# Delta rule by half blocks: the triangular inverse in 64 × 64 tiles, the pair loop unrolled and its order changed

## Chip, cores and metric

One core of one Trainium2 chip. The metric is the device time of one execution in microseconds (us); 0.2% of it, about 2.3 us, is what a measurement of this kernel can tell from no change.

## What is computed

Two transformer layers and a hybrid layer on 256 tokens of width 1024, all in float32. The change lies in one part of the hybrid layer, the gated delta rule (8 heads of 128):

```
q, k, v = silu(causal_dwconv(h @ w_q | h @ w_k | h @ w_v))    # four taps
g = -exp(a_log) * softplus(decay + dt);  beta = sigmoid(beta_logit)
q = l2norm(q) * dk ** -0.5;  k = l2norm(k);  G = cumsum(g)
m  = strict_lower((beta * k) @ k.T * exp(G_i - G_j))
sol = triangular_solve(m + I, [beta * v, beta * exp(G) * k])
u, w = sol
qk = lower(q @ k.T * exp(G_i - G_j))
# scan over chunks c:
v_new = u - w @ state;  o = exp(G) * q @ state + qk @ v_new
state = state * exp(G_last) + (k * exp(G_last - G)).T @ v_new
# then: rmsnorm(o, gain) * silu(z) @ w_branch_b
```

The kernel works in chunks of 128 tokens, two chunks per head, so that for each head two matrices I + m of 128 × 128 are inverted.

## The kernel before

Every projection splits a float32 weight chunk of 128 × 1024 into a high part (ScalarE, L343) and a low part (VectorE or GpSimd, L354, `raw - high`), and TensorE takes three matmuls of 256 columns (high·xh, high·xl, low·xh) for each 128 × 128 block: 24 matmuls make one projected block of 128 channels × 256 tokens. The delta rule's blocks are written at L1572 (`gdn_block`), in two parts of 12. Block (x, e) is query (x = 0), key (1), value (2) or gate z (3) of head e of a pair. ScalarE takes its last tap (L1587), VectorE adds three taps (L1607), ScalarE makes a tanh (L1598) into an SBUF buffer, and VectorE multiplies the two SBUF buffers to the silu (L1617). A gate block needs only a tanh (L1592) and one product (L1627). All low parts of this phase are GpSimd's.

The heads go in four pairs. `pair_pe` for pair i has two stages.

- **Levels.** The inverse is built by doubling: starting from blocks of 2, six levels each multiply M by the inverse (`level_x`, L1809, 4 matmuls, one for each of the pair's four matrices, into bank A[0]); VectorE masks it (`level_xm`, L1822); TensorE multiplies the masked product from both sides (`level_t`, L1816 and L1817, 8 matmuls into A[2] and A[3]); VectorE subtracts (`level_tt`, L1827, 1024 columns; L1830 at the last level). The inverse and its transpose are kept, each 128 × 512. A plain float32 matmul is two passes on TensorE, so that the trace shows 8 and 16 instructions. Behind each of the 12 groups stands half a block of the next pair: (0,0), (1,0), (2,0), (0,1), (1,1), (2,1) in the 12 gaps.
- **Tail.** The transposes of the next pair's queries and keys (`turn_pe`, L1640), the recurrence f1 to f4 (L1847 to L1879), and between its steps the blocks (3,0) and (3,1), the next pair's values transposed (L1647), the normed queries and keys turned back (`back_pe`, L1655), their products (L1667), the pair's result transposed (L1891), the next M transposed (L1676), and last `spin(pe, A[1], 4)`: four matmuls of 512 columns on constants (L491) whose result nobody reads.

Between them runs a chain over the other engines for the next pair: squares (ScalarE, L1682), their sums (VectorE, L1713), the root (GpSimd, `root_pool`, L1766), a factor and the normed rows (VectorE, `norm_dve`: L1732, L1734), back, copies (ScalarE, L1694), products, masks (VectorE, L1754), first inverse (GpSimd, `init_pool`: L1796, L1799; and VectorE, `init_dve`: L1761, L1762). The pair's own result norm (L2035, root at L2098, L2040, transpose, L2048) stands in the tail too. Each engine works its list in order. For the last pair the gaps hold attention's first projections (L2159, L2171). `gdn_pe` and its like are the ramp: the first pair's eight blocks, with the gates, before pair 0.

The pairs run as first pair, a hardware loop over the middle (`over`), last pair.

Of the kernel before, what the change touches and what calls it, by code (L numbers as in the profile page):

```python
# [19 lines left out]
ALU = mybir.AluOpType  # L20
# [3 lines left out]
P = 128  # L24
TOK = 256
# [17 lines left out]
LEVELS = 6  # L43

# [67 lines left out]
for _n, _w in (("ident", P), ("upper", P), ("strict_lower", P), ("level1", P), ("level1_t", P),  # L112
               ("levels", LEVELS * P), ("ones", P), ("causal", 3 * P), ("dist", NT * TOK),
               ("mla_cos", NT * MLA_ROPE), ("mla_sin", NT * MLA_ROPE), ("mla_rot", TOK),
               ("att_cos", NT * 2 * ROT), ("att_sin", NT * 2 * ROT)):
    _const(_n, _w)
# [3 lines left out]
def constants():  # L120
# [12 lines left out]
    def level(s):  # L133
        return (r // (2 * s) == k // (2 * s)) & (r % (2 * s) >= s) & (k % (2 * s) < s)

    put("level1", level(1))
    put("level1_t", level(1).T)
    put("levels", np.stack([level(2 << n) for n in range(LEVELS)], 1))
# [112 lines left out]
def build(nc, dram, y_out):  # L251
# [66 lines left out]
    def repeat(ap, n):  # L318

        return ap.unsqueeze(1).to_broadcast([P, n, ap.shape[1]])  # L320
# [1199 lines left out]
    tanh_ = [sb(f"tanh{x}", [P, TOK]) for x in range(4)]  # L1520
# [11 lines left out]
    qk_t = silu2[:, 0:4, :].rearrange("p (e x) (c k) -> p e (x c) k", e=2, c=2)  # L1532
    qdec_t = sb("qdec_t", [P, 2, P])
# [4 lines left out]
    inv = sb("inv", [P, 2, 4, P])  # L1538
    bm = sb("bm", [P, 2, 4, P])
    dcum = bm[:, 0, :, :]  # L1540
    xm = sb("xm", [P, 4, P])
# [10 lines left out]
    level_of = cst("levels", "p (l k) -> p l k", l=LEVELS)  # L1552
    BLOCKS = [(0, 0), (1, 0), (2, 0), (0, 1), (1, 1), (2, 1)]
# [5 lines left out]
    def gdn_block(pe, x, e, j, part):  # L1559
# [3 lines left out]
        if part == 0:  # L1563
            chunk_ready(pe, p, slot, c)
            if not (isinstance(b_, int) and b_ == 0):
                pe.wait_ge(taps[x]["tap"], 3 * b_ if x < 3 else b_)
            elif x == 3:
                pe.wait_ge(z_["dve"], 10)
# [7 lines left out]
    def block_act(act, split, x, e, j):  # L1576
        block_mid_act(act, split, x, e, j)
        block_end_act(act, x, e, j)

    def block_mid_act(act, split, x, e, j):  # L1580
# [3 lines left out]
        if x < 3:  # L1584
            if not (isinstance(b_, int) and b_ == 0):
                act.wait_ge(taps[x]["silu"], b_)
            act.activation(conv[x][:], W[x][:, 0:TOK], ACT.Copy, scale=conv_tap(b_, x, 3)).then_inc(taps[x]["mid"], 1)  # L1587
            refill(split, p, slot, c)
        else:
            if not (isinstance(b_, int) and b_ == 0):  # L1590
                act.wait_ge(taps[x]["tap"], b_)
            act.activation(tanh_[x][:], W[x][:, 0:TOK], ACT.Tanh, scale=0.5).then_inc(taps[x]["th"], 1)  # L1592
            refill(split, p, slot, c)

    def block_end_act(act, x, e, j):
        if x < 3:
            act.wait_ge(taps[x]["tap"], 3 * (2 * j + e) + 3)
            act.activation(tanh_[x][:], conv[x][:], ACT.Tanh, scale=0.5).then_inc(taps[x]["th"], 1)  # L1598
# [13 lines left out]
    def block_silu_dve(dve, x, e, j):  # L1612
        b_ = 2 * j + e
        dve.wait_ge(taps[x]["th"], b_ + 1)
        if (x, e) == BLOCKS[0] and not is0(j):
            dve.wait_ge(e_["grown"], j)
        dve.scalar_tensor_tensor(silu2[:, 3 * e + x, :], tanh_[x][:], 1.0, conv[x][:], ALU.add, ALU.mult).then_inc(taps[x]["silu"], 1)  # L1617

    def block_dve(dve, x, e, j):
        b_ = 2 * j + e  # L1620
        if x < 3:
            block_taps_dve(dve, x, e, j)
            block_silu_dve(dve, x, e, j)
        else:
            dve.wait_ge(taps[x]["th"], b_ + 1)
            dst = z2[:, b_, :] if isinstance(b_, int) else z2[:, bass.ds(b_, 1), :].rearrange("p a k -> p (a k)")
# [1104 lines left out]
```

## Time and profile before

| | us |
|---|---|
| median of 3 runs (1140.10 to 1142.44) | 1141.54 |
| profiled execution, own time | 1142.67 |
| its span in the trace | 1140.8 |
| TensorE busy (95% of the span) | 1084.0 |
| VectorE busy (61%) | 695.8 |
| ScalarE busy (49%) | 560.6 |
| GpSimd busy (37%) | 427.7 |
| mean granted TensorE clock | 0.988 |

The profiled execution is 1.1 us over the median. Busy time counts each record from start to its modelled end; matmuls overlap, so starts are the better measure of their cost. In the trace's lines a float32 matmul counts as two instructions; PEld is the weight load.

### The profile page before, as it was taken

Reading aid. Unit: us, or ns where it says so; the run is one execution under the profiler, and the core shown is the slowest. Engines: PE = TensorE matmul, PEld = TensorE weight load, DVE = VectorE, ACT = ScalarE, POOL = GpSimd, SP = SyncE. Lnnn points to the kernel's source line nnn. Section 1 sums busy time; section 2 is a strip of 40 time slices with the busy share of each in tenths; the row PEclk is TensorE's granted clock in tenths of the full one; section 3 lists DMA queues with packets and bytes.
Section 4 is the critical chain, followed back from the end, with each engine's and each line's share of the span. In section 5 each row is a group of like instructions: output and inputs, shape, how many; then the busy total and the mean of one; then the engine's idle time right before and its main releaser. Section 6 shows DMA issues by size and latency. Waiting matters only on the chain.

```text
span 1140.8 us, 21023 instructions
## 1 busy us (share of the span) xinstructions
PE 1084.0 (95%) x7774; PEld 991.4 (87%) x7774; DVE 695.8 (61%) x1054; ACT 560.6 (49%) x1022; POOL 427.7 (37%) x295
## 2 busy tenths in 40 slices
PE   9799999999999998999999987999999999999997
PEld 7699689999969986799999876888898989999996
DVE  3555776776676556677676666666667455544444
ACT  4455665555555555655555554233323245544442
POOL 1000233334332331333334636546564345534331
PEclk9999999999999999999999998999999999999999
DMA  8234366555435422555564323131220324446551
GB/s 341 84 110 137 129 206 217 185 186 182 148 130 169 147 96 109 200 190 184 177 208 160 130 95 112 45 104 49 100 82 29 120 85 148 153 142 204 184 183 38
DMA packets 46129, 162.43 MB, mean 142 GB/s; under 512 B 5248, under 2 KB 5504, under 8 KB 45952
## 3 DMA queue, kind: packets, MB, share of 16 engines
q1 hardware_dynamic: 44784, 157.05, 41.3%
q0 software_dynamic: 1296, 4.72, 1.3%
q8 instruction: 32, 0.52, 0.2%
q14 instruction: 17, 0.14, 0.0%
HBM read 160.70 MB, written 1.05 MB: 142 GB/s over the span
## 4 chain that ended last, share of the span: by engine, by line
PE 83%; DVE 9%; ACT 3%; issue 2%; POOL 2%; DMA 0%; DVEq 0%; POOLq 0%; ACTq 0%
PE work L385 13%; PE work L387 13%; PE work L386 13%; PE acc L385 5%; PE acc L386 5%; PE acc L387 5%; PE work L1572 5%; PE work L2159 4%; PE work L2171 2%; PE acc L1809 2%; DVE silu L1617 2%; PE acc L1817 2%; PE acc L2171 1%; DVE conv L1607 1%; PE acc L1816 1%
## 5 line engine op out<-in xcount | busy, mean ns | idle before, releaser
L354 POOL TENSOR_TENSOR low<-raw,high 128x1024 fp32r<-128x1024 f32 x109 | 265.3, 2436 | 328.3 <-ACT high L343 328.3
L354 DVE TENSOR_TENSOR low<-raw,high 128x1024 fp32r<-128x1024 f32 (+3 forms) x183 | 271.1, 1489 | 163.7 <-ACT high L343 163.5
L343 ACT ACTIVATE high<-raw 128x1024 fp32r<-128x1024 f32 (+2 forms) x293 | 300.1, 1032 | 44.0 <-DMA raw<-in_w_out 22.1
L385 PE MATMUL work<-xh,high 128*128 128x256 f32 (+1 forms) x1032 | 292.3, 283 | 0.7 <-DVE low L354 0.7
L386 PE MATMUL work<-xl,high 128*128 128x256 f32 (+1 forms) x1032 | 289.4, 280 | 0.0
L387 PE MATMUL work<-xh,low 128*128 128x256 f32 (+1 forms) x1032 | 289.1, 280 | 0.0
L385 PEld LDWEIGHTS work<-xh,high 128*128 128x128 f32 (+1 forms) x1032 | 194.5, 188 | 7.6 <-issue 4.8
L386 PEld LDWEIGHTS work<-xl,high 128*128 128x128 f32 (+1 forms) x1032 | 194.8, 189 | 2.3 <-issue 0.6
L387 PEld LDWEIGHTS work<-xh,low 128*128 128x128 f32 (+1 forms) x1032 | 194.8, 189 | 0.2
L1110 POOL TENSOR_TENSOR h<-gelu,cv 128x256 f32<-128x256 f32 x44 | 48.8, 1108 | 200.6 <-ACT gelu L1030 106.8
L1572 PE MATMUL work<-xh,high 128*128 128x256 f32 x256 | 77.2, 301 | 3.4 <-DVE conv L1607 1.7
L1572 PE MATMUL work<-xl,high 128*128 128x256 f32 x256 | 72.4, 283 | 0.0
L1572 PE MATMUL work<-xh,low 128*128 128x256 f32 x256 | 72.3, 282 | 0.0
L385 PE MATMUL acc<-high,hh 128*128 128x512 f32 x168 | 65.9, 392 | 1.2 <-DVE low L354 1.2
L386 PE MATMUL acc<-low,hh 128*128 128x512 f32 x168 | 65.8, 392 | 0.0
L387 PE MATMUL acc<-high,hl 128*128 128x512 f32 x168 | 65.4, 389 | 0.0
L1036 ACT ACTIVATE hh<-h 128x256 fp32r<-128x256 f32 x44 | 18.4, 418 | 70.1 <-POOL h L1110 70.1
L1572 PEld LDWEIGHTS work<-xh,high 128*128 128x128 f32 x256 | 49.3, 193 | 4.0 <-issue 3.1
L1024 ACT ACTIVATE cv<-work,vec 128x256 f32<-128x256 f32 x44 | 24.8, 564 | 51.0 <-PE work L387 51.0
L1572 PEld LDWEIGHTS work<-xl,high 128*128 128x128 f32 x256 | 49.3, 192 | 0.0
L1572 PEld LDWEIGHTS work<-xh,low 128*128 128x128 f32 x256 | 49.0, 191 | 0.0
L1112 POOL TENSOR_TENSOR hl<-h,hh 128x256 fp32r<-128x256 f32 x44 | 34.0, 773 | 24.4 <-ACT hh L1036 24.4
(376 smaller groups left out, 2345.5 us busy)
## 6 DMA issues: line engine op xcount, KB each, us to landing
raw<-in_w_ffn SPq DMA_DIRECT2D x132, 512.0 KB, 4.2
raw<-in_w_out SPq DMA_DIRECT2D x39, 512.0 KB, 4.1
raw<-in_w_diff SPq DMA_DIRECT2D x32, 512.0 KB, 4.2
raw<-in_w_att SPq DMA_DIRECT2D x32, 512.0 KB, 3.9
raw<-in_w_gdn SPq DMA_DIRECT2D x24, 512.0 KB, 3.7
raw<-in_w_mla SPq DMA_DIRECT2D x8, 512.0 KB, 3.3
raw<-in_w_gdnz SPq DMA_DIRECT2D x8, 512.0 KB, 5.0
raw<-in_w_mla SPq DMA_DIRECT2D x8, 384.0 KB, 3.2
```

The costliest lines, as they stand in the source:

```text
L343: act.activation(high[k][:, 0:w], raw[k][:, 0:w], ACT.Copy).then_inc(high_done[k], 1)
L354: eng.tensor_tensor(low[k][:, 0:w], raw[k][:, 0:w], high[k][:, 0:w], ALU.subtract).then_inc(low_done[k], 1)
L385: pe.matmul(out, lhs[0], rhs[0], start=start, stop=False)
L386: pe.matmul(out, lhs[0], rhs[1], start=False, stop=False)
L387: return pe.matmul(out, lhs[1], rhs[0], start=False, stop=stop)
L1024: act.activation((cg, cv)[value][j][:], W[bank][:, 0:TOK], ACT.Identity, scale=ffn_taps(layer, i, j, value, 1, 0), bias=ffn_taps(layer, i, ...
L1110: pool.tensor_tensor(h32[j][:], gelu[j][:], cv[j][:], ALU.mult).then_inc(s["h32"], 1)
L1112: pool.tensor_tensor(hl[j][:], h32[j][:], hh[j][:], ALU.subtract).then_inc(s["hl"], 1)
L1572: last = pe.matmul(W[x][:, 0:TOK], l[slot][:, b * P:(b + 1) * P], r[:, b, :], start=(s == 0), stop=(s == 23))
L1617: dve.scalar_tensor_tensor(silu2[:, 3 * e + x, :], tanh_[x][:], 1.0, conv[x][:], ALU.add, ALU.mult).then_inc(taps[x]["silu"], 1)
L2159: last = pe.matmul(W[0][:, t * TOK:(t + 1) * TOK], x[:, b, t * P:(t + 1) * P], w[k][:, o:o + TOK], start=(b == 0 and term == 0), stop=(b = ...
L2171: last = pe.matmul(out, w[k][:, b * P:(b + 1) * P], x[:, b, :], start=(s == 0), stop=(s == 23))
```

## The change

1. The inverse's diagonal 64 × 64 blocks are built alone. `inv` shrinks from 128 × 2 × 4 × 128 to 128 × 2 × 4 × 64, both halves on their own partitions. In `level_x` and `level_t` each 128 × 128 × 128 matmul becomes two of 64 × 64 × 64 (rows and outputs on partitions 0 to 63, and on 64 to 127). Five levels go that way; a last one makes the off-diagonal 64 × 64 block, with 4 + 4 matmuls of that size, into `inv_t`, the full transposed inverse. Products of both sides go into one bank.
2. Order on TensorE: gaps hold (0,0), (1,0), (0,1), (1,1), (3,0), (2,0). `turn_pe` moves up to gap 9, ahead of the last level. Values are transposed at gap 2 of the pair's own levels, the result of the pair before at gap 5. The tail holds block (3,1) (between f1 and f3), `back_pe` behind f2, products behind f3, `turn_m_pe` and then block (2,1). The spin is gone; the ramp's last spin is 2 instead of 4.
3. VectorE: the result norm's three steps move to levels 1, 2 and 3 or 4 of the next pair, scaled keys and values to levels 0 and 4, z's products and the masks to the tail. `init_pool` becomes VectorE's `init_rows_dve`. The taps stand between a level's two VectorE steps, the silu behind the second.
4. The tanh of a query, key or value block is written to the free half of the block's own PSUM bank; the next block in that bank then waits for the silu, not for the taps.
5. Pairs are unrolled in Python on all engines; the weight loads on the sync queue are written out in the new order.

```diff
 def gdn_block(pe, x, e, j, part):
-                pe.wait_ge(taps[x]["tap"], 3 * b_ if x < 3 else b_)
+            elif x < 3:
+                pe.wait_ge(taps[x]["silu"], b_)
...
-            act.activation(tanh_[x][:], conv[x][:], ACT.Tanh, scale=0.5).then_inc(taps[x]["th"], 1)
+        act.activation(W[x][:, TOK:2 * TOK], conv[x][:], ACT.Tanh, scale=0.5).then_inc(taps[x]["th"], 1)
...
 def level_x(pe, l, j):
         for c in range(4):
-            last = pe.matmul(A[0][:, c * P:(c + 1) * P], mt[:, c, :], inv[:, 0, c, :], start=True, stop=True)
+            at = slice(c * HALF, (c + 1) * HALF)
+            if l < LEVELS - 1:
+                for h_ in HALVES:
+                    last = pe.matmul(A[0][h_, at], mt[h_, c, h_], inv[h_, 0, c, :], start=True, stop=True)
+            else:
+                last = pe.matmul(A[0][upper, at], mt[lower, c, upper], inv[lower, 0, c, :], start=True, stop=True)
 def level_t(pe, l, j):
-                pe.matmul(A[2][:, c * P:(c + 1) * P], inv[:, 1, c, :], xm[:, c, :], start=True, stop=True)
-            last = pe.matmul(A[3][:, c * P:(c + 1) * P], xm[:, c, :], inv[:, 1, c, :], start=True, stop=True)
+                for h_ in HALVES:
+                    pe.matmul(A[2][h_, at], inv[h_, 1, c, :], xm[h_, c, :], start=True, stop=True)
+                for h_ in HALVES:
+                    last = pe.matmul(A[2][h_, at_t], xm[h_, c, :], inv[h_, 1, c, :], start=True, stop=True)
+            else:
+                last = pe.matmul(A[2][lower, at], xm[upper, c, :], inv[upper, 1, c, :], start=True, stop=True)
 def level_tt(dve, l, j):
+            if l == LEVELS - 2:
+                dve.wait_ge(e_["tt"], LEVELS * j + l + 1)
+                for h_ in HALVES:
+                    dve.tensor_copy(inv_t[h_, :, h_], inv[h_, 1, :, :])
+def init_rows_dve(dve, j):
+        for h_ in HALVES:
+            last = dve.tensor_tensor(bm[h_, 0, :, 0:HALF]..., mk[h_, :, 0, :, h_], level1..., ALU.mult)
+        dve.tensor_tensor(inv[:, 0, :, :], repeat(cst("ident_half"), 4), bm[:, 0, :, 0:HALF], ALU.subtract)
+def gap_pe(pe, i, gap):
+            gdn_block(pe, *GAP_BLOCKS[gap // 2], i + 1, gap % 2)      # attention's gaps for the last pair
+        if gap == 2:
+            turn_values_pe(pe, i)
+        if gap == 5 and i > 0:
+            turn_result_pe(pe, i - 1)
+        if gap == 9 and not last_pair:
+            turn_pe(pe, i + 1)
 def pair_pe(pe, i):                     # tail, more pairs to come
-            gdn_block(pe, 3, 0, i + 1, 0)
+            gdn_block(pe, 3, 1, i + 1, 0)         # behind f1
-            gdn_block(pe, 3, 0, i + 1, 1)
+            back_pe(pe, i + 1)                    # behind f2
+            gdn_block(pe, 3, 1, i + 1, 1)
-            turn_values_pe(pe, i + 1)
-            back_pe(pe, i + 1)
+            products_pe(pe, i + 1)                # behind f3
-            gdn_block(pe, 3, 1, i + 1, 0)
-            products_pe(pe, i + 1)
-            gdn_block(pe, 3, 1, i + 1, 1)
+            turn_m_pe(pe, i + 1)                  # behind f4
+            for part in range(2):
+                gdn_block(pe, 2, 1, i + 1, part)
-            turn_m_pe(pe, i + 1)
-            spin(pe, A[1], 4)
 def pair_pool(pool, i):
+            root_pool(pool, i + 1)
+            block_low_pool(split, 3, 0, i + 1)
+            block_low_pool(split, 2, 0, i + 1)
+            pool.wait_ge(e_["init_g"], i + 2)
+            grow_pool(pool, i + 1)
+            block_low_pool(split, 3, 1, i + 1)
+            block_low_pool(split, 2, 1, i + 1)
+        else:
+            refill(split, ph["att"], 0, 0)
+            result_root_pool(pool, i - 1)
```

## Rows read from the trace of the kernel before

**Rows 1.** Windows: ramp, pair 0, pair 1; start:end, length, busy (count) by engine, clock, DMA.
```profile
668.10:717.90 49.80, 40.29 (x284) 36.27 (x283) 34.51 (x52) 25.50 (x42) 31.42 (x19) 0.93 0.24 85
717.90:774.30 56.40, 52.82 (x413) 49.51 (x412) 36.72 (x57) 19.37 (x35) 27.87 (x20) 0.97 0.23 75
774.30:829.20 54.90, 51.25 (x413) 47.93 (x413) 36.74 (x57) 19.38 (x35) 30.98 (x21) 1.00 0.24 77
```

**Rows 2.** TensorE's waits in pairs 1 and 2 (774 to 883.5 us): total, times, longest.
```profile
PE work L1647 <- DVE silu L1617: 3.8, 2, 1.9
PE work L1655 <- DVE qk_tok L1734: 1.5, 2, 0.7
PE acc L1809 <- DVE inv L1762: 1.1, 2, 0.6
```

**Rows 3.** TensorE's timeline, one level of pair 1: start, length, engine, line, tiles, shapes, count.
```profile
785.66 1.16 PE L1809 MATMUL acc<-inv,mt 128*128 128x128 f32 x8
786.58 0.36 PE L1572 MATMUL work<-xh,high 128*128 128x256 f32 x1
...
788.07 0.38 PE L1816 MATMUL acc<-xm,inv 128*128 128x128 f32 x2
...
789.78 0.36 PE L1572 MATMUL work<-xh,high 128*128 128x256 f32 x1
...
791.33 0.38 PE L1809 MATMUL acc<-inv,mt 128*128 128x128 f32 x1
```

**Rows 4.** TensorE's timeline: matmuls with 64 weight rows (L1199) and their neighbours; 128 rows (L856).
```profile
406.78 1.06 PE L1231 MATMUL work<-v_sb,prob_t 128*128 128x128 f32 x8
407.76 1.13 PE L1199 MATMUL work<-k_sb,q_pair 64*128 64x256 f32 x8
...
409.05 0.28 PE L386 MATMUL work<-xl,high 128*128 128x256 f32 x1
```
```profile
40.98 0.59 PE L856 MATMUL work<-kr_t,qr_t 128*128 128x256 f32 x2
41.42 0.59 PE L855 MATMUL work<-k_sb,q_sb 128*128 128x256 f32 x2
```

**Rows 5.** Line L1199 in 407.70 to 407.80 us: durations in ns, first and last start.
```profile
L1199 PE MATMUL work<-k_sb,q_pair x2: 480/480/480, 407.8 to 407.8; 64*128 64x256 f32 x2
```

**Rows 6.** TensorE's timeline: the closest starts of two full-size matmuls.
```profile
38.46 0.22 PE L385 MATMUL work<-high,ckh 128*128 128x128 f32 x1
38.52 0.28 PE L386 MATMUL work<-low,ckh 128*128 128x128 f32 x1
```

**Rows 7.** TensorE's timeline, end of pair 1's tail.
```profile
825.03 3.60 PE L491 MATMUL acc<-const 128*128 128x512 f32 x8
829.19 1.16 PE L1809 MATMUL acc<-inv,mt 128*128 128x128 f32 x8 [0.56 <-DVE inv L1762]
```

**Rows 8.** VectorE's timeline in pair 1's tail.
```profile
810.10 1.22 DVE L1713 TENSOR_REDUCE ssq<-sq 128x8 f32<-128x1024 f32 x1 [2.00 <-ACT sq L1682]
...
813.43 2.41 DVE L1617 SCALAR_TENSOR_TENSOR silu<-tanh,conv 128x256 f32<-128x256 f32 x1 [0.48 <-ACT tanh L1598]
...
815.95 1.29 DVE L1734 TENSOR_TENSOR qk_tok<-work,fac 128x512 f32<-128x512 f32 x2
```

**Rows 9.** GpSimd's timeline in the same stretch.
```profile
811.61 1.64 POOL L1766 TENSOR_TENSOR root<-mean,vec 128x8 f32<-128x8 f32 x1 [4.38 <-DVE mean L1714]
813.22 2.34 POOL L354 TENSOR_TENSOR low<-raw,high 128x1024 fp32r<-128x1024 f32 x1
821.37 1.01 POOL L2098 TENSOR_TENSOR root<-mean,vec 128x4 f32<-128x4 f32 x1 [5.81 <-DVE mean L2036]
```

**Rows 10.** GpSimd's timeline in the last pair, whose third level begins at 894.65.
```profile
896.41 2.37 POOL L354 TENSOR_TENSOR low<-raw,high 128x1024 fp32r<-128x1024 f32 x1 [10.42 <-ACT high L343]
```

**Rows 11.** The ramp: VectorE's timeline, and TensorE's longest wait.
```profile
694.68 2.18 DVE L1617 SCALAR_TENSOR_TENSOR silu<-tanh,conv 128x256 f32<-128x256 f32 x1
```
```profile
PE work L1640 <- DVE silu L1617: 4.6, 1, 4.6
```

More of the change, by code:

```diff
@@ L1519, in build @@
               "xm tt x t f1 f1ev f2 f2ev f3 f3ev f4 osq oss om oroot on ot o32 oh ol chain")
-    tanh_ = [sb(f"tanh{x}", [P, TOK]) for x in range(4)]
+    tanh_z = sb("tanh_z", [P, TOK])
     conv = [sb(f"conv{x}", [P, TOK]) for x in range(3)]
@@ L1735, in norm_dve, with scaled_keys_dve @@
         last.then_inc(e_["tk"], 1)
[L1737 to L1740 removed]
+    def scaled_keys_dve(dve, j):
         if is0(j):
@@ new lines, in turn_result_pe @@
+    def turn_result_pe(pe, j):
+        pe.wait_ge(e_["on"], j + 1)
+        for c in range(4):
+            last = pe.transpose(A[3][:, c * P:(c + 1) * P], ogn[:, c, :], ident)
+        last.then_inc(e_["ot"], 1)
+    def gap_pe(pe, i, gap):
+        last_pair = i == PAIRS - 1
+        if last_pair:
+            if gap == 7:
+                pe.wait_ge(e_["tv"], PAIRS)
+            att_gap_pe(pe, gap)
+        else:
+            gdn_block(pe, *GAP_BLOCKS[gap // 2], i + 1, gap % 2)
[5 more added lines that the diff above has]
+            turn_pe(pe, i + 1)
@@ L1832, in pair_pe @@
     def pair_pe(pe, i):
-        more = not (isinstance(i, int) and i == PAIRS - 1)
+        more = i < PAIRS - 1
         for l in range(LEVELS):
-            for half in range(2):
-                (level_x, level_t)[half](pe, l, i)
-                gap = 2 * l + half
-                if more:
-                    gdn_block(pe, *BLOCKS[gap // 2], i + 1, gap % 2)
-                    if gap == 11:
-                        turn_pe(pe, i + 1)
-                else:
-                    att_gap_pe(pe, gap)
+            level_x(pe, l, i)
+            gap_pe(pe, i, 2 * l)
+            level_t(pe, l, i)
+            gap_pe(pe, i, 2 * l + 1)
@@ L1888, in pair_pe @@
                 att_gates(pe, 1, part)
-        pe.wait_ge(e_["on"], i + 1)
-        for c in range(4):
-            last = pe.transpose(A[0][:, c * P:(c + 1) * P], ogn[:, c, :], ident)
-        last.then_inc(e_["ot"], 1)
-        if more:
-            turn_m_pe(pe, i + 1)
-            spin(pe, A[1], 4)
+            turn_result_pe(pe, i)
     def block_pe(pe, x, e):
@@ L1995, in gdn_act, with result_mean_dve @@
         mt_act(act, 0)
-        over(act, PAIRS, lambda i: pair_act(act, i), 2)
+        block_high_act(act, split, 3, 1, 0)
+        for i in range(PAIRS):
+            pair_act(act, i)
+    def result_mean_dve(dve, j):
+        dve.wait_ge(e_["osq"], j + 1)
+        chain = Chain(dve, e_["oss"], 1, j)
+        chain(dve.tensor_reduce(ssq4[:], junk[:, 0:512].rearrange("p (a k) -> p a k", a=4), AX.X, ALU.add))
+        dve.tensor_scalar(mean4[:], ssq4[:], 1.0 / P, EPS, ALU.mult, ALU.add).then_inc(e_["om"], 1)
@@ L2048, in pair_dve @@
[L2048 to L2053 removed]
+        level_xm(dve, 0, i)
+        block_taps_dve(dve, 2, 1, i)
+        level_tt(dve, 0, i)
+        block_silu_dve(dve, 2, 1, i)
+        scaled_keys_dve(dve, i)
+        level_xm(dve, 1, i)
```

511 lines of the change are left out of this document (298 added, 213 removed).

## The prediction

> **What bounds the kernel now.** I read the page first, then windows over the phase that the change touches, then TensorE's waits and its timeline, and last the timelines of VectorE and GpSimd where TensorE waits for them. TensorE is busy for 95% of the span, and no other engine for more than 61%: what sets the end is TensorE's own list, plus the places where it waits. In the windows [rows 1] the ramp takes 49.8 us for 40.3 us of matmuls, pair 0 takes 56.4 us and pair 1 takes 54.9 us for about 51 to 53 us. So nearly all of a pair is matmuls; the ramp is not, it follows VectorE. The waits [rows 2] are few: (3.8 + 1.5 + 1.1) / 2 = 3.2 us in a pair, all in the tail, and they start with a silu of 2.41 us. Pair 0 has the same list as pair 1 and is 1.5 us longer at a granted clock of 0.97 against 1.00: one stretch at 1.2 GHz instead of 2.4 GHz, behind the tail's waits.
>
> The spin [rows 7] is 8 instructions from 825.03; the records' ends are modelled, so I take (3.60 − 0.16) = 3.44 us by starts. It is work for nobody, and even behind it TensorE waits another 0.56 us for the first inverse.
>
> **Term 1, the levels' matmuls.** Before, by starts in [rows 3]: a level's first group is 8 instructions and takes 0.92 us (0.89 us without the step to the next form), half a block takes 1.49 us, the second group is 16 instructions in 789.78 − 788.07 = 1.71 us (1.78 us at 0.111 each, which I take), and the level ends at 5.67 us. After, there are 16 and 32 instructions of 64 columns. What one costs no row shows. From below: the 128-column one takes 0.111 us, so half of it, 0.055 us; two in different halves of the array may run at once. That they do is seen at L1199: a 256-column float32 instruction on 128 rows takes (41.42 − 40.98) / 2 = 0.22 us, eight with 64 rows take 1.07 us to the next start, or 0.13 us each [rows 4], and two of them have one start [rows 5]. So I take pairs: 8 × 0.055 = 0.44 us and 16 × 0.055 = 0.88 us. But going in and out of such a form costs something: L1231's 8 instructions from 406.78 would be over at 407.67, and L1199 starts at 407.76 (0.09 us); its four steps of 0.215 and one of 0.117 us end at 408.74 while the second matmul behind it starts at 409.05 (0.31 us) [rows 4]. That is 0.40 us for each group, and a pair has 12 groups. A level becomes 0.84 + 1.28 us of groups against 0.89 + 1.78 us: 0.55 us less. The last level, 8 + 8 instructions in one quarter of the array, is 2 × (0.44 + 0.40) = 1.68 us against 1.78. In a pair 5 × 0.55 + 0.1 = 2.85 us, in four **−11.4 us**. Most of the halved work goes into the 0.40 us.
>
> VectorE's two steps of a level halve (512 and 1024 columns to 256 and 512). It has then about 3.3 us of work with taps and silu in a level of about 4.9 us; I cost its levels at nothing for TensorE, since half a block (1.49 us) covers each step. Without that cover each of the two steps would show by its 0.4 to 0.7 us.
>
> **Term 2, the spin.** Three pairs lose 3.44 us, **−10.3 us**, since block (2,1), 2.8 us of needed work taken out of a gap, stands in its place; all other moved TensorE work (values' and result's transposes, 0.44 us each) only changes place.
>
> **Term 3, old waits.** The silu that took 2.41 us read two SBUF operands and began just behind a GpSimd low part (813.22 for 2.34 us) and ended just behind it [rows 8, 9]. With its tanh in PSUM it should take about 0.5 us, and it is no longer in the chain. The three waits go: −3.2 us a pair, **−9.6 us**, and the slow-clock stretch of pair 0 (−1.5 us) may go with them or come back elsewhere; I leave it out of the sum.
>
> **Term 4, new waits**, in a pair, from what stands ahead in each engine's list. (a) `turn_pe` at gap 9 wants the silu of block (1,1), which stands behind the fourth level's subtraction and two new SBUF copies; the copies meet GpSimd's masks. The subtraction can start 3.7 us into the level and takes about 0.7, copies 0.6 to 1.3, silu 0.5: 5.5 to 6.2 us against 4.9: 0.9 us. (b) The chain from there: transposes 0.9, squares 1.2, z's silu 0.4, sums 1.22 [rows 8], root 1.64 [rows 9]. It now runs beside the last level and f1. Behind the root GpSimd goes straight on to the low part of (3,0), which has long been ready, 2.34 us; the factor L1732, a small product of two SBUF tiles, wants to start at the same moment. If it is held as the silu was, the normed rows come 2.3 + 1.29 us behind the root and `back_pe` waits 1.5 us; if not, nothing. I take 1.5, because the silu that began 0.2 us behind a low part was held for all of it. (c) `init_dve`'s last step, again SBUF only, comes just as GpSimd begins the low part of (3,1): 0 to 2.3 us late, of which block (2,1) hides about 1.2; I take 1.2. Sum 3.6 us a pair, **+10.8 us**.
>
> **Term 5, the last pair.** GpSimd's first job there is the low part of attention's second chunk, which ends at 898.8, 4.1 us into the third level [rows 10]; the result's root is now queued behind it (+1.0, as L2098 [rows 9]), and VectorE's list holds the norm (0.7) ahead of the third level's subtraction, which TensorE wants 4.9 us into the level. 4.1 + 1.0 + 0.7 + 0.7 = 6.5: **+1.6 us**.
>
> **Term 6, the ramp.** Five of its silus take 1.2 to 2.7 us, of which one is shown [rows 11]; at 0.5 us they give VectorE 7.8 us back, and the shorter spin 1.7 us. Against it: block (0,1) now waits for the silu of (0,0), which stands behind the gates' first steps, and (1,1) for that of (1,0), 3.9 and 2.6 us of TensorE idle early on; the 4.6 us wait at L1640 goes. Walking the lists through with the durations of the same instructions I come to a first level 5 to 6 us earlier; **−5 us**, and −2 to −8 as bounds.
>
> **Sum.** −11.4 − 10.3 − 9.6 + 10.8 + 1.6 − 5 = −23.9 us on the profiled execution's 1142.7: 1118.8; the median lies 1.1 us lower, **1118 us** (−2.1%). Loop branches that go with the unrolling, and later instruction loads, I cost at nothing: under 0.5 us in either direction, by the absence of any such wait among [rows 2].
>
> **Rivals.**
>
> *Fewer new waits* (15%). If small SBUF products on VectorE aren't held by GpSimd's low parts, (b) and (c) fall away, 3 × 2.7 = 8.1 us, and with pair 0's clock 1.5 more: 1108. For it: the sizes are tiny. Against: rows 8 and 9.
>
> *The halves don't run together* (20%). L1199's two halves write two PSUM banks; the new ones write one bank on different partitions. If they take turns, groups are 16 × 0.055 + 0.40 and 32 × 0.055 + 0.40 us, 0.44 + 0.88 = 1.3 us more for each of 20 levels, +26 us; about 3 us of it would cover new waits: 1141, no change. The Trainium skill, in TensorEngine Tiling (Array Packing), section Restrictions and Gotchas, says that different row tiles cannot access the same PSUM bank simultaneously; by it this rival is what happens. No row here tests it, since the rows' halves differ in bank too.
>
> *Slower: a small matmul has a floor* (13%). The change doubles the count, 120 to 240 in the five full levels of a pair, 480 to 960 in all four. The closest starts of two full-size matmuls anywhere are 0.06 us apart [rows 6], and no row has a sustained rate better than 0.11 us. If an instruction costs at least 0.06 us whatever its size, pairs or not, the groups are 16 × 0.06 + 0.40 = 1.36 and 32 × 0.06 + 0.40 = 2.32 us, 1.56 us more in each of 20 levels, +31 us: 1149; at 0.111 us, +82 us: 1200. It decides from a mean of about 0.052 us on, where 960 × (p − 0.0275) equals the 24 us of the sum. Against it: two starts together in [rows 5].
> The Trainium skill, in TensorE: Matmul & The Clock Gate, section on the back-to-back issue gap, gives about 62 ns per matmul where the sequencer's microcode decodes it; by that figure this rival's price would be 960 × 0.034 = 33 us and the time 1151.
>
> *The tail's chain needs the spin's time* (12%). If what now covers the first inverse is 3 to 4 us short in each pair, 1128.
>
> **How the numbers follow.** My own case has 40%, with a range of its own of 1111 to 1125; the rivals as given. The range takes in the first, the fourth and the second rival, and leaves the floor and the tails of the others out: 1105 to 1143. Faster by more than 0.2% (below 1139.2): 0.40 + 0.15 + 0.12 + a third of 0.20 + 0.02 = 0.76; within it: 0.11; slower: 0.13.
>
> **What would show it.** Level groups: starts from the first L1809-like matmul to the next block, 0.84 us, and 1.28 us for the second; if the first takes 1.3 us the halves take turns. A pair: 47.5 us or so. TensorE's waits: behind the silu of (1,1) at the transposes, behind the normed rows at `back_pe`, behind the inverse at level 0. L1732's successor: 0.15 us or over 2 us. The ramp's first level at about 50 − 5 us from its start, with the silus near 0.5 us. What would make it wrong: another price of the 64 × 64 form, or of going into it; and more stretches at the lower clock, 1.5 us each, if half-filled tiles count for less as activity.

## The result, and the profile after

The kernel after takes **1114.55 us** (median of 4 runs, 1114.01 to 1116.95); before, on the same chip, 1140.92 (1140.10 to 1142.44). The ratio is 0.977, 95% interval 0.975 to 0.979: faster, 3.4 us below the forecast of 1118 and inside its range of 1105 to 1143. Profiled execution against profiled execution it is 1116.95 against 1142.67 us, spans of 1114.8 and 1140.8.

The windows of the kernel after, cut as in [rows 1]: the ramp, from the first block of queries to the first level, and pairs 0, 1 and 2.
```profile
667.70:719.60 51.90, 39.52 (x277) 36.46 (x275) 26.76 (x50) 25.52 (x41) 24.77 (x15) 0.90 0.22 72
719.60:767.20 47.60, 44.56 (x520) 41.63 (x521) 31.70 (x60) 18.65 (x34) 25.49 (x16) 0.96 0.29 90
767.20:813.70 46.50, 43.49 (x524) 40.56 (x525) 34.31 (x64) 19.65 (x36) 27.36 (x17) 1.00 0.30 92
813.70:859.10 45.40, 43.41 (x526) 40.57 (x526) 33.25 (x65) 17.69 (x33) 22.70 (x15) 1.00 0.22 71
```
Pairs 0 and 1 fell from 56.4 and 54.9 us to 47.6 and 46.5, and pair 2 from 54.1 to 45.4: 25.9 us for the three. The ramp grew by 2.1 us, at a granted clock of 0.90 against 0.93. What lies behind pair 2 is 1.7 us shorter, what lies ahead of the ramp 0.4 us. That is all of the 26.0 us between the two spans.

TensorE's timeline of one level in pair 0 at full clock, as in [rows 3]; a group of the second kind is broken into eight records, of which the first and the last are shown.
```profile
731.34 0.68 PE L1839 MATMUL acc<-inv,mt 64*64 64x64 f32 x16
731.96 0.38 PE L1590 MATMUL work<-xh,high 128*128 128x256 f32 x1
...
733.56 0.33 PE L1853 MATMUL acc<-xm,inv 64*64 64x64 f32 x4
...
734.43 0.28 PE L1855 MATMUL acc<-inv,xm 64*64 64x64 f32 x4
...
736.25 0.68 PE L1839 MATMUL acc<-inv,mt 64*64 64x64 f32 x16
```
By starts a first group takes 0.62 us. The second one's records of 4 instructions start 0.117 us apart, 0.029 us for one; the group takes 1.08 us. One by one, the instructions of the two halves start in pairs 0.007 us apart, a pair every 0.058 us. A level takes 4.91 us against 5.67.

TensorE's waits from pair 1's first level to pair 3's (767.2 to 859.1 us), against [rows 2]: total, times, longest.
```profile
PE work L1673 <- DVE qk_tok L1751: 2.3, 2, 1.1
PE acc L1839 <- DVE inv L1800: 2.2, 2, 1.1
PE work L1658 <- DVE silu L1639: 1.6, 2, 0.8
```
The three old waits and the spin of [rows 7] are gone. In their place stand three new ones of 1.1, 1.1 and 0.8 us. The one at L1839 is the first level's wait: it stands ahead of pairs 1 and 2 and not ahead of pair 3, the other two stand in all three pairs. VectorE's and GpSimd's timelines in pair 1's tail show what is behind two of them, as in [rows 8, 9].
```profile
799.16 2.35 DVE L1749 TENSOR_TENSOR fac<-root,vec 128x8 f32<-128x8 f32 x1 [1.34 <-POOL root L1804]
801.54 1.29 DVE L1751 TENSOR_TENSOR qk_tok<-work,fac 128x512 f32<-128x512 f32 x2
...
811.44 2.13 DVE L1800 TENSOR_TENSOR inv<-const,bm 128x256 f32<-128x256 f32 x1
```
```profile
797.49 1.64 POOL L1804 TENSOR_TENSOR root<-mean,vec 128x8 f32<-128x8 f32 x1 [0.54 <-DVE mean L1731]
799.10 4.69 POOL L357 TENSOR_TENSOR low<-raw,high 128x1024 fp32r<-128x1024 f32 x2
...
810.91 2.38 POOL L357 TENSOR_TENSOR low<-raw,high 128x1024 fp32r<-128x1024 f32 x1
```
A product of eight columns takes 2.35 us. It begins 0.06 us behind the start of GpSimd's low parts (two in a row, 4.69 us) and ends with the first of them. The step of the first inverse shown last begins 0.5 us behind the start of another low part and ends 0.3 us behind that part; ahead of pair 3 no low part is beside it, it takes 0.43 us, and the first level doesn't wait. The silus, which now read one operand from PSUM, take 0.42 us whatever GpSimd does.

The ramp, in TensorE's timeline (the steps with idle time ahead of them, in brackets) and in VectorE's.
```profile
677.45 0.36 PE L1590 MATMUL work<-xh,high 128*128 128x256 f32 x1 [3.55 <-DVE silu L1639]
...
684.37 0.35 PE L1590 MATMUL work<-xh,high 128*128 128x256 f32 x1 [2.54 <-DVE silu L1639]
...
702.89 0.55 PE L1590 MATMUL work<-xh,high 128*128 128x256 f32 x1 [3.42 <-DVE silu L1639]
```
```profile
672.82 1.84 DVE L1494 TENSOR_SCALAR gate_neg<-gate_z 128x16 f32<-128x16 f32 x1
674.69 2.27 DVE L1496 TENSOR_TENSOR gate_abs<-gate_z,gate_neg 128x16 f32<-128x16 f32 x1
676.89 0.41 DVE L1639 SCALAR_TENSOR_TENSOR silu<-work,conv 128x256 f32<-128x256 f32 x1
...
697.78 2.50 DVE L1739 TENSOR_TENSOR bm<-cum_all,gate_cum 128x512 f32<-128x512 f32 x1
```
Each of the three waits is for a silu of 0.42 us that stands in VectorE's list behind other work: behind the gates' steps of 1.84 and 2.27 us (16 columns each), behind the taps of block (0,1), and behind a decay step of 2.50 us. A fourth wait, 2.9 us, ends the ramp: the copy of the masks' transposes stands behind a high part that waited 4.2 us for its DMA, and the first inverse's last step is held again (1.29 us, beside a low part from 716.82).

### The profile page after: what moved, and what is told of

It is laid out like the page before. It is cut to its first block, busy times and chain, and to the rows that moved or that the text cites. A ratio compares the mean times of both kernels' runs of the same rounds, so it can differ in the third digit from the quotient of the medians.

```text
span 1114.8 us, 21844 instructions
## 1 busy us (share of the span) xinstructions
PE 1056.9 (95%) x8226; PEld 963.6 (86%) x8226; DVE 681.1 (61%) x1079; ACT 561.8 (50%) x1022; POOL 412.9 (37%) x283
## 4 chain that ended last, share of the span: by engine, by line
PE 83%; DVE 8%; POOL 3%; ACT 3%; issue 2%; DMA 1%; DVEq 0%; POOLq 0%; SPq 0%; ACTq 0%
PE work L388 13%; PE work L390 13%; PE work L389 13%; PE work L1590 6%; PE acc L388 5%; PE acc L389 5%; PE acc L390 5%; PE work L2299 4%; PE work L2311 2%; PE acc L2311 2%; PE acc L1839 1%; POOL low L357 1%; PE acc L1853 1%; ACT high L346 1%; PE acc L1855 1%
## 5 line engine op out<-in xcount | busy, mean ns | idle before, releaser
L1113 POOL TENSOR_TENSOR h<-gelu,cv 128x256 f32<-128x256 f32 x44 | 48.8, 1109 | 200.5 <-ACT gelu L1033 106.7
L1629 DVE SCALAR_TENSOR_TENSOR conv<-work,vec,conv 128x255 f32<-128x255 f32 (+2 forms) x72 | 34.5, 479 | 19.3 <-ACT conv L1600 17.6
```

Source lines behind the costliest of these rows:

```text
L1113: pool.tensor_tensor(h32[j][:], gelu[j][:], cv[j][:], ALU.mult).then_inc(s["h32"], 1)
L1629: dve.scalar_tensor_tensor(conv[x][:, back:TOK], W[x][:, 0:TOK - back], conv_tap(b_, x, 3 - back), conv[x][:, back:TOK], ALU.mult, ALU.add ...
```

## The experiments

Eleven kernels ran, on two chips, each beside the kernel before. Ratios are to the kernel before, whose medians there were 1140.2 to 1141.7 us. Runs of one kernel differ by up to 9 us (before: 1135.4 to 1144.9) with the mean granted clock (0.994 in the fastest, 0.987 in the slowest), so for small effects the lengths of the stretches in the trace say more than the medians. Here they are by starts, in us.

| kernel | from | median us | ratio (95%) | ramp | pairs 0, 1, 2 |
|---|---|---|---|---|---|
| before | | 1140.92 | | 49.8 | 56.4, 54.9, 54.1 |
| after | | 1114.55 | 0.977 (0.975 to 0.979) | 51.9 | 47.6, 46.5, 45.4 |
| halves apart | after | 1140.95 | 1.000 (0.998 to 1.002) | 52.2 | 56.2, 53.6, 51.3 |
| blocks only | before | 1131.08 | 0.992 (0.989 to 0.995) | 49.0 | 52.9, 54.3, 53.2 |
| no spin | before | 1148.33 | 1.006 (1.004 to 1.008) | 49.8 | 54.8, 58.1, 57.4 |
| spin back | after | 1122.47 | 0.984 (0.981 to 0.987) | 51.8 | 49.9, 48.8, 48.8 |
| GpSimd later | after | 1108.59 | 0.972 (0.969 to 0.975) | 52.0 | 43.6, 44.0, 44.0 |
| copies later | after | 1111.58 | 0.975 (0.972 to 0.977) | 51.6 | 47.5, 46.1, 44.3 |
| ramp, early silus | after | 1111.92 | 0.975 (0.972 to 0.978) | 48.4 | 47.6, 46.5, 45.4 |
| ramp, whole | after | 1107.28 | 0.971 (0.968 to 0.974) | 42.4 | 46.2, 46.5, 45.4 |
| all orders | after | 1095.15 | 0.961 (0.959 to 0.963) | 43.6 | 46.4, 43.0, 43.0 |
| keys in ramp | all orders | 1094.56 | 0.960 (0.957 to 0.963) | 42.4 | 42.6, 43.0, 43.0 |
| ramp, gates | keys in ramp | 1094.60 | 0.959 (0.956 to 0.963) | 44.0 | 42.6, 43.0, 43.0 |

**Halves apart.** Do the two 64 × 64 halves run together?
```diff
 def level_x(pe, l, j):
-        for c in range(4):
-                for h_ in HALVES:
-                    last = pe.matmul(A[0][h_, at], mt[h_, c, h_], inv[h_, 0, c, :], start=True, stop=True)
+        for h_ in (HALVES if l < LEVELS - 1 else (upper,)):
+            for c in range(4):                    # the same in level_t
+                last = pe.matmul(A[0][h_, at], mt[h_, c, h_], inv[h_, 0, c, :], start=True, stop=True)
```


> From the kernel after; the order of the matmuls in a level is changed alone, all of the lower half's first and then all of the upper half's, so that no two neighbours lie in different quarters of the array. In the trace of the kernel after, four 64 x 64 instructions take 0.117 us by starts, 0.029 us each. Theory A (neighbours in two quarters run together, each takes 0.058 us by itself): groups of 16 grow from 0.61 to about 1.08 us and groups of 32 from 1.08 to about 2.0 us, 1.4 us more in each of 20 levels, +28 us, less some 3 us that covers present waits: +20 to +28 us against the kernel after. Theory B (a 64-column instruction simply costs 0.029 us, nothing runs together): no group changes, +0 us within 0.2%.

It is 26.4 us slower than the kernel after, by nothing but the order of the same instructions. TensorE's timeline of a level:
```profile
731.42 0.96 PE L1839 MATMUL acc<-inv,mt 64*64 64x64 f32 x16
...
733.92 0.32 PE L1853 MATMUL acc<-xm,inv 64*64 64x64 f32 x2
734.09 0.28 PE L1854 MATMUL acc<-inv,xm 64*64 64x64 f32 x2
...
734.67 0.33 PE L1853 MATMUL acc<-xm,inv 64*64 64x64 f32 x4
...
737.35 0.96 PE L1839 MATMUL acc<-inv,mt 64*64 64x64 f32 x16
```
Now two instructions start every 0.117 us, 0.058 for one, where four did; only where the list goes from one half to the other are there four (734.67). The level takes 5.93 us. That is +1.02 us in 20 levels, 20.4 us. TensorE's waits in the three pairs grow by 2.3 us (the one for the silu at L1658 from 0.8 to 2.7, 2.7 and 1.6, the one at L1673 stays in one pair only), and the rest goes with the clock (0.91 in pair 0's window, 0.97 in pair 1's, for 0.96 and 1.00). Theory A holds: the halves run together, though both write one PSUM bank.

**Blocks only.** The inverse alone, without the order around it. The first step of the rows' inverse is made on VectorE here, as in the kernel after, and TensorE's pairs are unrolled.
```diff
-        over(pe, PAIRS, lambda i: pair_pe(pe, i))
+        for i in range(PAIRS):
+            pair_pe(pe, i)
...
             masked_dve(dve, i + 1)
+            init_rows_dve(dve, i + 1)
...
-            init_pool(pool, i + 1)               # with it, level_x, level_t, level_xm, level_tt as after
```


> From the kernel before; only the inverse by 64 x 64 blocks with its constants, inv_t, the first step of the rows' inverse on VectorE instead of GpSimd, and TensorE's pairs unrolled. The order of the work, tanh in SBUF, the masks and the spin stay as before. Theory A (the levels' matmuls are on TensorE's path and come out at the groups seen in the kernel after, 0.61 and 1.08 us for 0.89 and 1.78): 0.76 us less in each of 20 levels and 0.5 us in each of four last levels, -17 us, 1124 us, with the waits of the tail unchanged at about 3.2 us a pair. Theory B (the shorter levels take away cover and half comes back as waits in the gaps or in the tail): -8 us, 1133 us, and new waits in the table of waits. Theory C (the 64 x 64 form costs what the prediction priced, 0.84 and 1.28 us a group): -11 us.

10.6 us faster by the medians, where the levels alone give 17. Its waits from pair 1's first level to pair 3's (against [rows 2]), and VectorE's timeline in the tail:
```profile
PE acc L1822 <- DVE inv L1773: 6.1, 2, 3.1
PE work L1656 <- DVE silu L1626: 3.8, 2, 1.9
PE work L1664 <- DVE qk_tok L1743: 1.3, 2, 0.7
```
```profile
814.41 1.55 DVE L1804 TENSOR_TENSOR bm<-mk,const 64x256 f32<-64x256 f32 x2
816.00 2.49 DVE L1808 TENSOR_TENSOR inv<-const,bm 128x256 f32<-128x256 f32 x1
...
820.28 1.37 DVE L1773 TENSOR_TENSOR inv<-const,bm 128x256 f32<-128x256 f32 x1
```
The first two lines are the rows' inverse, 4.0 us that GpSimd made in the kernel before and that now stand in VectorE's list ahead of L1773. L1808 and L1773 moreover meet GpSimd work (a low part from 815.86 for 2.35 us, the result's low part from 819.89 for 1.47). The wait at the first level grows from 0.6 to 3.1 us ahead of pairs 1 and 2 and from none to 1.0 ahead of pair 3, 6.0 us in all, and behind the two long ones the first level takes 6.40 us instead of 4.92, at the lower clock (0.97 and 0.94 in the windows of pairs 1 and 2). The levels themselves come out as theory A has them: the other four are 4.9 us each, no wait appears in the gaps, and the two waits ahead in the tail are as before. So the size is nearer to theory B, but its reason, cover that shorter levels take away, is not what the trace shows: the moved steps and their holds are. In the kernel after the rows' steps stand on VectorE too, with no GpSimd step beside them (0.85 and 0.43 us in pair 1's tail), and block (2,1) stands ahead of the wait.

**The spin, from both sides.**
```diff
 # no spin, from before                       # spin back, from after
             turn_m_pe(pe, i + 1)                         turn_m_pe(pe, i + 1)
-            spin(pe, A[1], 4)               +            spin(pe, A[0], 4)
                                                          for part in range(2):
                                                              gdn_block(pe, 2, 1, i + 1, part)
```


> From the kernel before; only the spin of 8 instructions (3.44 us by starts) between the tail and the next pair's first level is taken out in the three pairs that have it. Theory A (it was cover: the first inverse is not ready before): TensorE waits at the first level for about 3.4 + 0.6 = 4 us instead, time within 0.3% of before, possibly with one more stretch at 1.2 GHz behind each wait (1.5 us each, up to +5 us). Theory B (the term of the prediction taken by itself: three times 3.44 us of needless work): -10 us.

> From the kernel after; the spin of 8 instructions is put back between the transposes of the masked keys and block (2,1) in each of three pairs, writing a bank that nobody reads there. It separates the spin from the block that took its place. Theory A (the time of the spin is a full loss where a block of needed work stands behind it, as the prediction's second term takes it): 3 x 3.44 = 10.3 us, less the 1.1 us a pair that TensorE waits at the first level now and that the spin would cover: +7 to +10 us. Theory B (what the spin covers is waits that the tail has anyway): 0 to +3 us.

Without the spin the kernel before is 6.6 us *slower*. TensorE's waits ahead of pairs 1, 2 and 3, and the windows of pairs 1 and 2, in that kernel:
```profile
PE acc L1809 <- DVE inv L1762: 11.2, 3, 4.0
```
```profile
771.90:830.00 58.10, 51.04 (x405) 49.76 (x405) 36.74 (x57) 19.37 (x35) 30.95 (x21) 0.94 0.21 73
830.00:887.30 57.30, 50.99 (x404) 49.70 (x404) 36.21 (x58) 18.54 (x34) 27.79 (x19) 0.94 0.16 55
```
TensorE waits 3.7 us a pair (4.0 at most) where it ran the spin for 3.44 and waited for at most 0.56, and behind each wait the first level takes 7.25 us instead of 5.66: the clock is 0.94 in both pairs where it was 1.00. That is theory A, and somewhat more than its 5 us: idle time was dearer here than needless work. Put back into the kernel after, the same spin costs 7.9 us: three times 3.44, less the wait of 1.1 us ahead of pairs 1 and 2 that it covers (the tails grow by 2.3, 2.3 and 3.4 us). That is theory A too. The spin's time could be had only because block (2,1), needed work, took its place.

**GpSimd later.** Does GpSimd's low part hold VectorE's small steps?
```diff
+            pool.wait_ge(e_["tk"], i + 2)
             block_low_pool(split, 3, 0, i + 1)
...
             grow_pool(pool, i + 1)
+            pool.wait_ge(e_["init_v"], 2 * (i + 1) + 2)
             block_low_pool(split, 3, 1, i + 1)
```


> From the kernel after; GpSimd waits for the normed rows before it makes the low part of block (3,0) and for both first inverses before that of (3,1), so that neither meets VectorE's small SBUF steps. In the kernel after the factor L1749 takes 2.35 us and the inverse's first step L1800 2.13 us, each for as long as a low part runs, and TensorE waits 1.1 us at L1673 and 1.1 us at L1839 in a pair. Theory A (VectorE is held by GpSimd's low part): both steps fall to about 0.15 to 0.3 us, both waits go or nearly so, 3 x 2.2 = 6.6 us less at most, some of it taken by the wait that is late next: -4 to -6.6 us against the kernel after. Theory B (the two steps are long for a reason of their own, or TensorE's waits come from elsewhere): their durations and the time stay, 0 us.

6.0 us faster. The durations of the factor's line and of the first inverse's last step, first in the kernel after (minimum/median/maximum in ns, four instructions, the first in the ramp), then here, and the only wait left in pairs 1 and 2:
```profile
L1749 DVE TENSOR_TENSOR fac<-root,vec x4: 700/2348/2354, 704.2 to 845.7; 128x8 f32<-128x8 f32 x4
...
L1800 DVE TENSOR_TENSOR inv<-const,bm x4: 426/1711/2133, 718.2 to 858.0; 128x256 f32<-128x256 f32 x4
```
```profile
L1749 DVE TENSOR_TENSOR fac<-root,vec x4: 168/168/697, 703.2 to 838.1; 128x8 f32<-128x8 f32 x4
...
L1800 DVE TENSOR_TENSOR inv<-const,bm x4: 424/425/1305, 717.0 to 849.0; 128x256 f32<-128x256 f32 x4
...
PE work L1658 <- DVE silu L1639: 1.6, 2, 0.8
```
2.35 us becomes 0.17, and both waits are gone, with the slower clock of pair 0 (0.96, now 1.00). Theory A. The stretches of the three pairs are 7.9 us shorter, of which 5.6 are the waits and 1.5 that clock; the medians' 6.0 us is less. The same low parts are still made, only a step of VectorE's later, and nobody waits for them.

The Trainium skill, in SBUF — State Buffer, section Who interferes with whom, says that a VectorE instruction with two SBUF inputs contends with a GpSimd instruction that reads SBUF, over a pair of ports that one of them holds alone, and that the order of issue decides which one blocks. The runs agree: 2.35 us against 0.17 for one instruction with and without a low part beside it, and 0.41 to 0.43 us for every silu since one of its inputs is in PSUM. The hold is not for two SBUF inputs alone: L1731, with one, takes 0.80 us for 0.17 in the next experiment.

**Copies later.**
```diff
             block_silu_dve(dve, 1, 1, i + 1)
+            whole_dve(dve, i)                # the two copies into inv_t, till now in level_tt
             scaled_values_dve(dve, i)
```


> From the kernel after; the two copies of the inverse's diagonal blocks into the 128-column form are made behind the silu of (1,1) instead of ahead of it. In the kernel after they take 0.38 and 0.68 us, and the transposes of queries and keys wait 0.8 us for that silu in each of three pairs. Theory A (the prediction's new wait a: the copies hold the silu up): the wait goes, 3 x 0.8 us = -2.4 us. Theory B (the wait only moves to the chain behind it, which the GpSimd's low part of (3,0) holds anyway): -0 to -1 us, the wait for the normed rows grows.

The wait of 0.8 us is gone from all pairs. In pair 2 nothing takes its place (44.3 us for 45.4). In pair 1 the wait for the normed rows grows from 1.1 to 1.8 us (pair 46.1 us for 46.5), because the chain's step ahead of the root now meets another GpSimd step, the result's low part:
```profile
792.37 0.80 DVE L1731 TENSOR_SCALAR mean<-ssq 128x8 f32<-128x8 f32 x1
...
838.50 0.17 DVE L1731 TENSOR_SCALAR mean<-ssq 128x8 f32<-128x8 f32 x1
```
The first is pair 1's, the second pair 2's. Theory A holds for pair 2, theory B in pair 1. In pair 0 a longer stretch at the lower clock (0.94 for 0.96) takes the gain back. The pairs give 1.5 us together, the medians 3.0; the intervals don't tell these apart.

**The ramp.**
```diff
+        block_silu_dve(dve, 0, 0, 0)
         gates_input_dve(dve)
-        block_silu_dve(dve, 0, 0, 0)
         block_taps_dve(dve, 1, 0, 0)
         gates_decay_dve(dve)
+        block_silu_dve(dve, 1, 0, 0)
         block_taps_dve(dve, 0, 1, 0)
-        block_silu_dve(dve, 1, 0, 0)             # end of "early silus"
...
+        squares_dve(dve, 0)
+        block_silu_dve(dve, 2, 0, 0)
         decay_dve(dve, 0)
-        squares_dve(dve, 0)
-        block_silu_dve(dve, 2, 0, 0)             # ScalarE: z_tanh_act before decay_act,
...                                               # mt_act before block_high_act(2, 1)
+        pool.wait_ge(e_["init_v"], 2)            # GpSimd: low part of (2,1) behind grow_pool
```


> From the kernel after; two moves in VectorE's list of the ramp alone: the silu of (0,0) ahead of the gates' first three steps, and the silu of (1,0) ahead of the taps of (0,1). In the kernel after block (0,1) waits 3.6 us for the first silu, which stands behind two small gate steps of 1.84 and 2.27 us, and block (1,1) waits about 2.5 us for the second, whose tanh is done at about 680.5 and which runs at 683.8. Theory A (the ramp follows these silus): the first wait falls below 0.7 us; block (1,1) starts when its silu allows, 3.5 us earlier than now; everything after it 3.5 us earlier, -3.5 us. Theory B (the ramp is set by the gates' chain or by GpSimd's low parts, which stay where they are): the waits move to another place and the first level starts where it does now, 0 to -1 us.

> From the kernel after; the two moves of the previous kernel, and in the second half of the ramp: VectorE makes the sums of squares and the silu of (2,0) ahead of the decays, ScalarE the tanh of (3,0) ahead of the decays' exponentials and the masks' transpose's copy ahead of the high part of (2,1), and GpSimd the low part of (2,1) only behind the first inverse. In the kernel after block (2,1) waits 3.4 us for a silu that stands behind a decay step of 2.50 us, and the first level waits 2.9 us for an inverse. Theory A (order within the lists of VectorE, ScalarE and GpSimd makes the ramp 51.9 us): 3.5 us as in the previous kernel, 3.4 us at block (2,1) and 1 to 2 us at the first level, -7 to -9 us against the kernel after, ramp 43 to 45 us. Theory B (the chain of sums, root, normed rows and products is late next and takes the place of the silus): -3.5 to -5 us, with a wait at the transposes of the normed rows.

The first takes 3.5 us off the ramp, as theory A had it, the second 9.5 us. With the second TensorE's waits in the ramp are:
```profile
PE work L1590 <- DVE silu L1639: 4.2, 2, 3.5
...
PE work L1590 <- POOL low L357: 0.8, 1, 0.8
...
PE acc L1839 <- DVE inv L1800: 0.4, 1, 0.4
```
The waits at block (2,1) and at the first level are gone or down to 0.4 us, and no wait for the normed rows appears: theory A. The 3.5 us left are for the silu of (1,0), behind the gates' exponential and logarithm on ScalarE.

**All orders, and two steps more.** All orders is GpSimd later, the whole ramp, copies later, and the result's root ahead of the low part in the last pair. Keys in ramp adds the first pair's `scaled_keys_dve` behind `norm_dve` in the ramp. Ramp, gates moves taps and silu of (1,0) ahead of the gates' absolute value and block (2,0) ahead of the gates' sums.

> From the kernel after; all orders tried so far together: GpSimd's two waits ahead of the low parts of (3,0) and (3,1), both parts of the ramp, the copies behind the silu of (1,1), and in the last pair the result's root ahead of the low part of attention's second chunk. Theory A (the waits are independent, each one is worth itself): -6 us for GpSimd's waits as measured, -7 to -9 for the ramp, less 1 us that both take from the first level, -2.4 for the copies, -0.9 for the root: -15 to -17 us against the kernel after, 1098 to 1100 us. Theory B (they share covers: where one wait goes the next is behind it): -10 us, 1105 us.

> From the kernel with all orders together; the first pair's two scaled keys, small products of two SBUF tiles, are made in the ramp behind the normed rows instead of behind the first level's silu. In the kernel with all orders they take 2.67 and 2.56 us in pair 0, for as long as three of GpSimd's low parts run on end, and TensorE waits 2.3 us for the second level's masked product and then runs for a while at the lower clock: pair 0 takes 46.4 us, pairs 1 and 2 take 43.0. Theory A (held by GpSimd, as the factor and the first inverse were): pair 0 falls to about 43 us, -3.4 us, 1092 us. Theory B (moved, they are held in the ramp and hold up the masked keys there): the ramp grows by what pair 0 gains, 0 us.

> From the kernel before this one (first pair's scaled keys in the ramp); in the ramp the taps and the silu of (1,0) go ahead of the gates' absolute value on VectorE, the tanh of (1,0) and the first step of (0,1) ahead of the gates' exponential and logarithm on ScalarE, and block (2,0) ahead of the gates' sums on TensorE. What is left of waits in the ramp is 3.4 us at block (1,1) for the silu of (1,0), whose tanh stands behind the gates' exponential and logarithm and their table loads. Theory A (that wait goes and the gates' chain, 2.3 us later, hides behind (2,0)): -3 us. Theory B (the gates' chain, through sums, rows and decays, is what the ramp really hangs on, and it is now later): 0 to +3 us, with a wait at the gates' sums or rows.

All orders take 19.4 us off the kernel after, more than theory A's 15 to 17; by the stretches it is 16.5 (ramp 8.3, pairs 7.1, last pair 1.1), and 1.7 us of the difference between the profiles lies ahead of the ramp, where the two kernels are the same. Pairs 1 and 2 are at 43.0 us, all of it busy TensorE. Pair 0 was not: VectorE's and GpSimd's timelines there show the same hold again.
```profile
713.97 2.67 DVE L1760 TENSOR_TENSOR kdec<-qk_tok,gate_kd 128x256 f32<-128x256 f32 x1
716.57 2.56 DVE L1761 TENSOR_TENSOR kbg<-qk_tok,gate_bg 128x256 f32<-128x256 f32 x1
```
```profile
711.64 7.21 POOL L357 TENSOR_TENSOR low<-raw,high 128x1024 fp32r<-128x1024 f32 x3 [3.05 <-ACT high L346]
```
Made in the ramp, they take 0.52 and 0.95 us, and pair 0 falls from 46.4 to 42.6 us; the windows of ramp and pairs with it:
```profile
666.90:709.30 42.40, 36.99 (x278) 33.83 (x277) 24.17 (x52) 23.55 (x39) 23.15 (x14) 0.96 0.25 86
709.30:751.80 42.50, 42.50 (x520) 40.05 (x520) 27.38 (x58) 19.52 (x34) 25.79 (x16) 1.00 0.32 103
751.80:794.90 43.10, 43.10 (x527) 40.56 (x526) 30.82 (x64) 19.68 (x35) 27.58 (x18) 1.00 0.33 99
794.90:837.90 43.00, 43.00 (x527) 40.49 (x526) 30.21 (x64) 18.73 (x34) 24.48 (x16) 1.00 0.22 74
```
The medians give only 0.6 us for that step, and the intervals of the two kernels overlap: all orders' profiled execution was its slowest (1098.8 of 1094.6 to 1098.8 us), so how much of pair 0's 3.8 us a usual execution loses is open. Moving the gates gave nothing. The wait for the silu of (1,0) goes, as theory A had it, but 1.6 us of wait for a low part take its place there, and at block (2,1) a wait of 3.4 us for a silu comes back. The ramp is 1.6 us longer: theory B in size, with the wait at another place than it named.

## Why the prediction was right, and where it was not

**Term 1, the levels, −11.4 forecast; right mechanism, price too high.** Halves that run together were right, and so was 0.029 us an instruction (0.0275 taken). The step in and out of the form was taken as 0.40 us a group from L1199. Counted as there, from the last matmul ahead of a group to the second one behind it, it is 0.34 us: 0.09 ahead, 0.62 − 16 × 0.029 = 0.15 inside, and 0.10 behind. The 128 × 128 groups had 0.17 and 0.01 us of such steps too, 0.09 a group, which the sum put at nothing, so that the change adds 0.25 us a group and not 0.40. A level, by starts, gains 5.67 − 4.91 = 0.76 us instead of 0.55, and the last one, with two groups of 0.61 us for 1.78, 0.56 instead of 0.1: 20 × 0.76 + 4 × 0.56 = −17.4 us.

**Term 2, the spin, −10.3; held**, with the reason that was given: block (2,1) in its place. Put back it costs 7.9 us net of the wait it covers.

**Term 3, old waits, −9.6; held.** All three are gone. They were 9.0 us, since the first level's 0.6 us stood ahead of pairs 1 and 2 only and the sum took it three times. The slow-clock stretch left out of the sum stayed in pair 0 (0.96).

**Term 4, new waits, +10.8; held in kind and place**, at 0.8, 1.1 and 1.1 us for 0.9, 1.5 and 1.2. With (c) ahead of two pairs only that is +8.0 us. GpSimd later shows the cause of (b) and (c), copies later that of (a).

In three pairs these make −13.1 − 10.3 − 9.0 + 8.0 = −24.4 us, against 25.9 measured; with the prediction's own numbers it would have been −17.7.

**Term 5, the last pair, +1.6; size.** The result's transposes wait 0.9 us. The stretch from the last pair's first level to f1, by starts, went from 34.0 to 32.2 us: −4.4 by levels, +0.9 by the wait, +0.9 by two sets of transposes that now stand here. That is −2.6; 0.8 us of the difference I could not place.

**Term 6, the ramp, −5 with bounds −2 to −8; wrong in sign, +2.1.** The failed step is "walking the lists through with the durations of the same instructions". The two early waits came as forecast (3.55 and 2.54 us, for 3.9 and 2.6). But the 7.8 us that five silus were to give back did not come back whole, because the hold was not a property of the silus, and the walk kept the old durations of steps that now stand at other moments. It belongs to whatever SBUF step meets a low part. The decay step, in the kernel before and after (minimum/median/maximum in ns):
```profile
L1722 DVE TENSOR_TENSOR bm<-cum_all,gate_cum x4: 684/684/685, 701.4 to 834.7; 128x512 f32<-128x512 f32 x4
```
```profile
L1739 DVE TENSOR_TENSOR bm<-cum_all,gate_cum x4: 681/684/2505, 697.8 to 828.3; 128x512 f32<-128x512 f32 x4
```
Its 2.50 us are in the ramp, where it had run free before. With L1517 (0.95 us for 0.16) and L1749 (0.70 for 0.19) 3.1 us are held that were free. Two waits were not forecast, 3.42 us at block (2,1) and 2.9 us at the first level. That an order of the lists alone takes 9.5 us off shows the ramp's matmuls were never its bound.

So the small error of 3.4 us is luck and hides two larger ones: 6.0 us too little gained in the levels, 7.1 too much in the ramp. Of the rest, 2.8 is in term 4, 0.6 the other way in term 3 and 1.1 in term 5, and 1.9 in the pairs and ahead of the ramp beyond what the terms name; 1.3 us is that the profiled execution lies 2.4 us over its median, not 1.1.

**The rivals.** *Halves don't run together* is refuted by halves apart: with the halves taking turns the kernel takes 1140.95 us, almost the rival's 1141. That the two agree so closely is luck: the rival added 26 us to 1118 and took 3 off, the run adds 26.4 to 1114.55, of which 20.4 are the levels'. The Trainium skill's rule in TensorEngine Tiling (Array Packing), section Restrictions and Gotchas, that different row tiles cannot access one PSUM bank simultaneously, would have had it so. The measurement decides: two quarters of the array that lie in different rows and different columns write one bank on different partitions at a combined 0.029 us an instruction, against 0.058 by themselves. *A floor for small matmuls* of 0.06 us or more, pairs or not, is refuted by the 0.029 us. In a single quarter they come no closer than 0.058 us, which is also half of the 128-column one's 0.111, so a floor for one tile and proportion are not told apart. The Trainium skill's 62 ns for a matmul decoded by the sequencer's microcode (TensorE: Matmul & The Clock Gate, section on the back-to-back issue gap) does not bind here. *The tail's chain needs the spin's time* is true of the old order (no spin) and not of the new one. *Fewer new waits* did not happen by itself; GpSimd later makes it happen, and its 1108.6 us is near that rival's 1108, though from another starting point (6.0 us off 1114.55, not 9.6 off 1118).

## What to carry to other kernels

An elementwise step between SBUF tiles costs what GpSimd is doing beside it: read its time at the moment it will run, not off its old row, and where it is in the chain put GpSimd's long steps behind it, or one operand in PSUM. A spin in front of a wait is cover for the clock; take it out only with needed work in its place. When a helper's result frees a bank (a silu in place of the taps), its place in the list has to move up too, in the ramp as well as in the loop.

## What the hardware showed that was not expected

Going into a 64 × 64 form and out of it cost TensorE 0.34 us a group, against the 0.40 us read at L1199's 64-row form, and 128 × 128 groups between 256-column matmuls had 0.09 us of it already. Two halves of the array wrote one PSUM bank at twice the rate of one half. In the kernel without the spin, waits of up to 4.0 us, one a pair, went with a mean clock of 0.94 in two of three pairs; in the kernel after, waits of 0.8 to 1.1 us left it at 1.00 in pairs 1 and 2. An instruction of 8 columns took 0.17 or 2.35 us, depending only on whether a GpSimd step of 2.35 us had begun just before it.
